# A hybrid encoder block on one core: where the weight sums' steps stand in the load queue, which PSUM banks the first down tiles use, and what the loads of embedding rows wait for

## The reference

```
u = rms_norm(x); z = u @ w_in          # z: GLU a, GLU b, q, k, v, two gates
c = a * sigmoid(b); c = causal_depthwise_conv31(c); c = silu(layer_norm(c)); yA = c @ w_conv_out
yB = sliding_window_attention(rope(q), rope(k), v, sinks) @ w_attn_out     # chunks of 64, window 128
y = sigmoid(gA) * yA + sigmoid(gB) * yB
h = x + rms_norm(y @ w_out)
gate, val = split(rms_norm(h) @ w_up)  # 2 x 2816 columns
f = (gelu(causal_depthwise_conv3(gate)) * val) @ w_down
h = h + rms_norm(f)
h = h + (p @ w_ple) * sigmoid(h @ w_ple_gate)
```

## Time and profile before

| | |
|---|---|
| median of three runs | 2669.7 us |
| the profiled execution | 2667.9 us, span 2666.1 us |
| mean granted TensorE clock | 0.996 |
| TensorE matmul busy | 2626.8 us, 99% |
| VectorE busy | 1605.1 us, 60% |
| ScalarE busy | 807.7 us, 30% |
| GpSimd busy | 1536.9 us, 58% |
| DMA | 579.60 MB, mean 217 GB/s |

### The profile page before, as it was taken

The page is one execution under the profiler, slowest core; times in us unless marked ns, Lnnn a source line. Parts: engine busy times, 40 slices in busy tenths (PEclk is TensorE's granted clock), DMA queues, the critical chain, the costliest instruction groups (busy, mean ns, idle before and its releaser), DMA issues.

```text
span 2666.1 us, 32289 instructions
## 1 busy us (share of the span) xinstructions
PE 2626.8 (99%) x11772; PEld 2152.4 (81%) x11772; DVE 1605.1 (60%) x2211; ACT 807.7 (30%) x1405; POOL 1536.9 (58%) x1860
## 2 busy tenths in 40 slices
PE   9999999999999999999999999999999999999998
PEld 7888878887888778788888778887888888888887
DVE  8985879576966696767556601167745455401275
ACT  2542442444334443433322220023322222310021
POOL 6767333213320220489889843387988888743585
PEclk9999999999999999999999999999999999999999
DMA  7878887868786775455556674446444444754434
GB/s 289 296 255 324 288 310 254 292 232 303 274 290 231 283 279 214 153 169 168 171 184 207 220 279 162 158 149 243 160 159 149 166 142 167 261 194 149 166 131 171
DMA packets 275550, 579.60 MB, mean 217 GB/s; under 512 B 22976, under 2 KB 113344, under 8 KB 274752
## 3 DMA queue, kind: packets, MB, share of 16 engines
q1 hardware_dynamic: 244144, 493.64, 53.8%
q10 hardware_dynamic: 31248, 83.90, 8.2%
HBM read 422.25 MB, written 155.19 MB: 217 GB/s over the span
## 4 chain that ended last, share of the span: by engine, by line
PE 83%; DMA 8%; POOL 4%; DVE 2%; issue 1%; SPq 1%; ACT 1%; ACTq 0%; DVEq 0%
PE ps L1279 10%; PE ps L1502 10%; PE ps L1496 10%; PE ps L1498 9%; PE ps L1275 9%; PE ps L1276 9%; PE ps L1265 6%; PE ps L1267 6%; PE ps L1266 6%; DMA up_quad<-in_up_quads 4%; DMA w_stage<-in_weights 2%; PE ps L1315 1%; PE ps L1318 1%; POOL w_lo L724 1%; PE ps L1333 1%; PE ps L1334 1%
## 5 line engine op out<-in xcount | busy, mean ns | idle before, releaser
L724 POOL TENSOR_TENSOR w_lo<-w_stage,w_hi 128x256 fp32r<-128x256 f32 x1184 | 1005.9, 879 | 25.6
L720 POOL CAST w_hi<-w_stage 128x1024 fp32r<-128x1024 f32 (+2 forms) x320 | 358.2, 1119 | 571.9 <-DMA w_stage<-in_weights 363.1
L1496 PE MATMUL ps<-comb_hi,w_hi 128*128 128x512 f32 x1232 | 479.6, 389 | 1.8 <-DVE comb_lo L2038 1.5
L1498 PE MATMUL ps<-comb_lo,w_hi 128*128 128x512 f32 x1232 | 479.4, 389 | 0.0
L1502 PE MATMUL ps<-comb_hi,w_lo 128*128 128x512 f32 x1232 | 330.3, 390 | 1.6 <-POOL w_lo L724 1.6
L734 POOL TENSOR_TENSOR up_quad<-up_quad 128x128 f32<-128x128 f32 x88 | 43.2, 490 | 498.0 <-DMA up_quad<-in_up_quads 498.0
L1833 DVE SCALAR_TENSOR_TENSOR ps<-conv_in,col,ps 128x512 f32<-128x512 f32 x436 | 294.1, 747 | 0.8
L1275 PE MATMUL ps<-ring_hi,w_hi 128*128 128x512 f32 x704 | 274.6, 390 | 2.7 <-ACT acc L1090 2.6
L1276 PE MATMUL ps<-ring_lo,w_hi 128*128 128x512 f32 x704 | 274.5, 390 | 0.0
L1502 PEld LDWEIGHTS ps<-comb_hi,w_lo 128*128 128x128 f32 x1232 | 230.6, 188 | 52.3 <-POOL w_lo L724 4.4
L1496 PEld LDWEIGHTS ps<-comb_hi,w_hi 128*128 128x128 f32 x1232 | 231.3, 188 | 50.9 <-DVE comb_lo L2038 1.9
(11 more groups left out here) (257 smaller groups left out, 4605.4 us busy)
## 6 DMA issues: line engine op xcount, KB each, us to landing
w_hi<-split_weights SPq DMA_DIRECT2D x138, 512.0 KB, 3.9
w_lo<-split_weights SPq DMA_DIRECT2D x138, 512.0 KB, 5.0
w_stage<-up_sums SPq DMA_DIRECT2D x176, 256.0 KB, 3.1
w_stage<-in_weights SPq DMA_DIRECT2D x86, 512.0 KB, 4.9
w_stage<-in_up_raw SPq DMA_DIRECT2D x132, 256.0 KB, 3.0
w_stage<-in_weights SPq DMA_DIRECT2D x64, 384.0 KB, 3.4
split_weights<-w_hi SPq DMA_DIRECT2D x46, 512.0 KB, 2.9
split_weights<-w_lo SPq DMA_DIRECT2D x46, 512.0 KB, 4.3
```

Source lines behind the costliest of these rows:

```text
L720: nc.gpsimd.tensor_copy(w_hi[:, slot, 0:many], w_stage[:, slot, 0:many]).then_inc(w_hi_ready, 1)
L724: last = nc.gpsimd.tensor_tensor(w_lo[:, slot, k:end], w_stage[:, slot, k:end], w_hi[:, slot, k:end].bitcast(F32), ALU.subtract)
L1496: nc.tensor.matmul(ps[:, bank], w_hi[:, slot, first + k], comb_hi[i][:, k], start=start and k == 0, stop=False, skip_group_check=True)
L1498: nc.tensor.matmul(ps[:, bank], w_hi[:, slot, first + k], comb_lo[i][:, k], start=False, stop=False, skip_group_check=True)
```

## The change

Four edits.

1. The steps of the weight sums stand at the blocks from B_QKV to the last merge block (30 a chunk) and, for chunks 1 and 2, at the last four output blocks. The total of 88 steps is the same. In chunks 1 and 2 there are 34 places as before; in chunk 3 the last 20 steps start at the first query block.
2. The loads of low_b and high_b stand at positions 2, 6, 8 and 10 of the last merge instead of 3, 4, 5 and 6.
3. The first eight down tiles use eight banks: 2, 3, 4, 5 and then 6, 7, 0, 1. Tiles 4 to 7 wait for the last eviction of the embedding projection, tile 8 for the copy of tile 0, and from tile 12 on the rule is the old one.
4. Each load of two tiles of ple_b waits for the tiles of h_mix that lie in its place and those before them.

```
-SUM_AT_BLOCK = [n for n, (c, b) in enumerate(ORDER) if 1 <= c and B_GLU + 4 <= b < B_WO]
+SUM_AT_BLOCK = [n for n, (c, b) in enumerate(ORDER) if 1 <= c and (B_QKV <= b < B_WO or c < CHUNKS - 1 and B_WO + 4 <= b < B_WP)]
...
+        def down_bank(m):
+
+            return (DN_BANK + WP_BANK)[m] if m < 8 else DN_BANK[m % 4]
...
-                    if 3 <= at < 5:
-                        load_raw(low_b, 1, 0, at - 3, low_b_loaded)
-                    if 5 <= at < 7:
-                        load_raw(high_b, 1, H4, at - 5, high_b_loaded)
+                    if at in (2, 6):
+                        load_raw(low_b, 1, 0, at // 4, low_b_loaded)
+                    if at in (8, 10):
+                        load_raw(high_b, 1, H4, at // 2 - 4, high_b_loaded)
...
-                        sp.wait_ge(h3_mid, (c + 1) * KD_)
+                        sp.wait_ge(h3_mid, c * KD_ + 2 * j)
...
                 if m < 4:
                     pe.wait_ge(ft_ready, (a // 2 + 1) * NF)
+                elif m < 8:
+                    pe.wait_ge(ple_out, sum(len(projected(i)) for i in range(0, a + 2, 2)))
                 elif m - 4 < COPIED:
-                    pe.wait_ge(dn_first, a // 2 * COPIED + m - 3)
+                    pe.wait_ge(dn_first, a // 2 * COPIED + (m - 7 if m < 12 else m - 3))
```

More of the change, by code:

```diff
@@ L1089, in down_copies @@
                         dn_done(a, 0, j, s)
-                        copy(result(a + s)[:, j], ps[:, DN_BANK[DOWN_AT[0, j, s] % 4]], ACT.Copy).then_inc(dn_first, 1)
+                        copy(result(a + s)[:, j], ps[:, down_bank(DOWN_AT[0, j, s])], ACT.Copy).then_inc(dn_first, 1)
             def down_square(c, j):
@@ L1598, in down_tile @@
                 b = B_DN + q * KD_ + j
-                bank = ps[:, DN_BANK[m % 4]]
+                bank = ps[:, down_bank(m)]
                 rounded_there(c, b)
@@ L2151, in add_down @@
                 tile = result(a + s)[:, j]
-                V.tensor_tensor(tile, tile, ps[:, DN_BANK[m % 4]], ALU.add).then_inc(dn_acc, 1)
+                V.tensor_tensor(tile, tile, ps[:, down_bank(m)], ALU.add).then_inc(dn_acc, 1)
             def h3_tile(c, j):
```

## The result

The changed kernel takes 2633.34 us (median of four runs, 2631.81 to 2633.6). The kernel before, run beside it, takes 2668.72. The ratio is 0.9864, 95% interval 0.9851 to 0.9876: 35.4 us less, where 31.1 were forecast. Of the 5.3 us between it and the forecast of 2638.6, 1.0 is the kernel before, whose median beside it was 2668.72 and not 2669.7; 4.3 are the change.

What follows compares the result with a forecast made beforehand. TensorE's matmuls fill 99% of the span, so only its idle time and low clock can be won: 18.8 + 4.2 + 8.1 = 31.1 us off 2667.9 gives 2636.8, or 2638.6 beside the median of 2669.7; range 2634 to 2653 us.

Steps and rivals of the forecast that it cites:

- The cause in the mixer: GLU of chunks 1 to 3: steps make SyncE issue the query blocks' weights 6.2 us late, into the u_kept stores.
- (a): Query blocks: the burst of u_kept stores still catches them; a third to a half of 18.8 stays, 2645 to 2648; chance 0.16.
- (c): Mixer: the steps were not the cause, weights are late from DMA alone; 2657 us; chance 0.05.
- (d): Slower: a step takes more than a block's time anywhere; with 9.9 us in the query blocks, 2701 us; chance 0.03.
- (e): Whole kernel: waits only move, the next late load takes every freed stretch; within 5 us of 2669.7; chance 0.03.
- The term 18.8: GLU and query blocks, chunks 1 to 3: 13.2 us of stalls at L1265 go, and 5.6 us of low clock.
- 4.2: Fifth down tile: eight banks remove a wait of 2.6 us and 1.6 us of low clock behind it.
- The term 8.1: Gate blocks: waits of 7.7 us at L1315 and 0.4 us at L1275 go.
- That stall cost no clock: Gates: the stretch with their stall has clock 1.00, so no low clock was counted there.
- Edit 3's and edit 4's mechanisms: Down tiles: tile 4 no longer needs tile 0's copy. Gates: ple_b loads wait for 2, 4, 6, 8 tiles, not all eight.
- Rival (b): Gates: the stall returns two blocks later behind the output store's wait; 4 to 5 us of 8.1 stay, 2643; chance 0.12.
- The port rule: Output blocks: GpSimd and two-input VectorE instructions lock one port pair; could cost four steps' GpSimd time a chunk; sum unchanged.

Runs made afterwards that it cites:

- two further profiles: The kernel before, unchanged, profiled twice more: 2679.65 and 2672.01 us.
- edit 1 alone: The kernel before with only the steps of the weight sums moved out of the GLU: 0.9941, 15.7 us less.
- single edits: The kernel before with one item of the change's list at a time: the first 0.9941, the third 0.9993, the fourth 0.9960.

## Why the prediction was right in its steps and short in its sum

- **The cause in the mixer** was right: late issue by SyncE behind the steps, not the DMA load alone. With the steps back in the GLU the same 6.2 us of lateness returns in chunk 3, and the stalls in chunks 2 and 3; in chunk 1 they don't. Rivals (a), (c), (d) and (e) are out. One step did take 10.3 us, more than the 9.9 of (d), but a single one, and the slots cover it.
- **The term 18.8** was too small by 3.0. The failed step is the sum "all 13.2 us of stalls at L1265 go, and with them the low clock": it counts a stall as the idle time that the profile shows. Start to start, each costs 0.27 us more, hidden in busy time. Ten stalls were in the three chunks, the one of 0.02 us among them: 2.7 us. The low clock was right: the four stalls that have it behind them cost 1.6, 1.6, 2.5 and 1.6 us on top of that. The same holds for one stall at the down tiles (4.5 for 4.2) and five in the gates.
- **The term 8.1** has a second fault, a wait that was left out. The five stalls of the gates are shown as 8.75 us, not 8.1; this row of the kernel before stands in no sum of the prediction:

```profile
PE ps L1279 <- POOL w_lo L724: 0.6, 1, 0.6
```

With it and 5 x 0.27 the gates come to 10.1, as measured.
- **"That stall cost no clock"** was true of one execution and was taken as true of the kernel. In two further profiles, and with edit 1 alone, the gates' stalls did cost clock. It may also be why the single edits' times don't add up to the change's, 15.7 + 9.5 + 2 = 27 against 35.4: an edit that removes some stalls doesn't save the clock of the others. This isn't shown. Each of these four gains is known to within 3 to 4 us, and in the profiled executions the single edits gave 16.6 + 9.5 + 6.2 = 32.3 against 34.4. Nor does the change remove every stall that can cost clock. At the start of the kernel, behind a wait of 1.9 us at L1553 (L1558), three single edits and one of the two further profiles had low clock; the changed kernel has a wait of 1.8 us there, and none in its profile. Here are that stretch with edit 1 alone and in the changed kernel:

```profile
5.00:25.00 20.00, 18.10 (x56) 11.70 (x55) 16.50 (x25) 10.14 (x18) 11.96 (x15) 0.91 0.68 259
5.00:25.00 20.00, 17.94 (x64) 11.69 (x63) 18.22 (x28) 10.95 (x20) 12.01 (x15) 1.00 0.68 259
```

- **Edit 3's and edit 4's mechanisms** were right. Tile 4 runs on while the copy of tile 0 still waits for its store (until 1542.13 in the new trace, after 11.43 us). SyncE's wait at the ple_b loads fell from 25.4 us to 0.3:

```profile
SPq L563 <- DMA out_h<-acc: 8.2, 1, 8.2
...
SPq L680 <- DVE second_acc L2167: 0.3, 1, 0.3
```

- **Rival (b)** exists in small. The wait for the output store is now the longest there, 8.2 us. GpSimd's remainders come 0.14 to 0.24 us late four times, and once, by 0.75 us shown, at the start of the next projection. With the wait for the store one block later that last stall is gone. In all it costs 1.2 to 1.3 us net, not 4 to 5.
- **The two rules of the Trainium skill.** The stretch at the down tiles moved 383 GB/s over 15 us, loads and stores together. The Trainium skill, "DMA: Bandwidth & Descriptors", section "Specifications", lists about 358 GB/s as one core's limit to HBM; this trace went above it, and its value decides. The port rule of the Trainium skill, "SBUF — State Buffer", section "SBUF: two separate sides", could show in the output blocks. With and without steps there the mixer ends the same to within the 0.3 us that the two runs differ by from the start, so no such loss reached TensorE; whether VectorE or GpSimd lost time there isn't told by this.
- **The range** began at 2634 because no term was given an error upward. With the waits as shown (24.6 us), the low clock (7.2) and 0.27 us for each of 16 stalls (4.3) the sum is 36.1 us, less 0.6 at the start, 0.3 before the down tiles and 1.3 behind the gates: 33.9, where the two traces differ by 34.4. That the time fell out of the range by only 0.7 us, and not inside it, is in part chance: the kernel before was 1.0 us faster beside it than when the forecast was made. The sum that was 4 us short isn't chance.

## What to carry to other kernels

In a stream of overlapping matmuls, take the loss at a stall from start to start of the matmuls around it, not from the idle time shown, and add the low clock that other executions may have there. When one queue issues both the critical loads and others, look for the waits in it: moving a group of waits away from a burst of stores won 21.8 us here, though it saved no byte. Judge a small edit by the starts of the same matmuls in both traces, stage by stage, when executions of one kernel differ by more than the edit is worth.

## What the runs showed that was not expected

- Whether a stall of some 2 us is followed by a low clock changes from one execution to the next, at the same place and for the same length (2.17 us without, 2.15 with). The largest seen without it in the first profile was 3.66 us; from 3.7 us up every stall of these traces had it. Each low stretch ahead of the last matmul lasted 3.4 or 6.8 us.
- The spread of the times may come from this, which isn't shown. The kernel before ran from 2662.3 to 2673.7 us in 17 runs beside the single edits, 11.4 us apart, and from 2666.0 to 2672.3 in the four beside the changed kernel, which ran from 2631.8 to 2633.6. But the version with the later store wait, with no low clock before its last matmul in its profile, ran from 2633.0 to 2639.3, and the run of 2639.3 had a mean clock of 0.998.
- A stall in TensorE's stream costs 0.27 us beyond what is shown as idle, at eleven stalls of the kernel before; 154 inserted breaks gave 0.29 at the break.
